# A third weight chunk at the feed-forward entries, and all first modulation blocks on VectorE, in a two-block float32 kernel

## The reference

```python
def modulated_norm(x, g, shift, scale):
    return rmsnorm(x, g) * (1 + scale) + shift
def swiglu(h, wg, wu, wd):                      # wg, wu: 1024 x 2816, wd: 2816 x 1024
    return (jax.nn.silu(h @ wg) * (h @ wu)) @ wd
def first_block(x, c, ...):
    c_act = jax.nn.silu(c)
    for l in range(2):
        mod = (c_act @ w_ada[l] + b_ada[l]).reshape(b, 9, 1, 1024)   # w_ada[l]: 1024 x 9216
        sh1, sc1, g1, sh2, sc2, g2, sh3, sc3, g3 = [mod[:, i] for i in range(9)]
        h = modulated_norm(x, norm_g[l, 0], sh1, sc1)
        x = x + 0.5 * g1 * swiglu(h, ffn_wg[l, 0], ffn_wu[l, 0], ffn_wd[l, 0])
        x = x + g2 * mixer(modulated_norm(x, norm_g[l, 1], sh2, sc2))
        x = x + 0.5 * g3 * swiglu(modulated_norm(x, norm_g[l, 2], sh3, sc3), ...)
    return x
```

## Time and profile before

| what | value |
|---|---|
| median of 3 runs | 2608.23 us (2608.07 to 2612.12) |
| the profiled execution: its time, its span | 2614.62 us, 2613.0 us |
| TensorE matmul, weight load | 2478.3 us (95%), 2118.1 us (81%) |
| VectorE, ScalarE, GpSimd busy | 1630.6 us (62%), 1080.0 us (41%), 315.1 us (12%) |
| DMA | 479.26 MB, 183 GB/s over the span |

### The profile page before, as it was taken

How to read it: one execution, slowest core, us unless ns; L and a number is a source line. 1 busy time by engine, 2 the same in 40 slices (tenths; PEclk the granted TensorE clock), 3 DMA queues, 4 the chain that set the end, 5 groups by cost and what they waited for, 6 DMA issues and landing times.

```text
span 2613.0 us, 35873 instructions
## 1 busy us (share of the span) xinstructions
PE 2478.3 (95%) x13317; PEld 2118.1 (81%) x13317; DVE 1630.6 (62%) x1759; ACT 1080.0 (41%) x1223; POOL 315.1 (12%) x425
## 2 busy tenths in 40 slices
PE   7999988999999899999998999899999999998998
PEld 7777857887888788888798888788788898887886
DVE  3887347767875555555566675645545657757455
ACT  3434335435434444444353334344344344254443
POOL 3110111101102000000005500000100016200000
PEclk9999979999999999999999999999999999999999
DMA  7996318967974466556543233556456331534554
GB/s 288 320 329 224 132 33 279 306 218 278 325 257 146 152 227 208 176 182 201 156 122 97 99 114 139 168 189 213 148 193 218 94 108 62 164 114 145 178 191 145
DMA packets 337379, 479.26 MB, mean 183 GB/s; under 512 B 19867, under 2 KB 280314, under 8 KB 337258
## 3 DMA queue, kind: packets, MB, share of 16 engines
q1 hardware_dynamic: 314458, 398.43, 46.6%
q0 software_dynamic: 22800, 79.23, 8.2%
HBM read 476.55 MB, written 1.05 MB: 183 GB/s over the span
## 4 chain that ended last, share of the span: by engine, by line
issue 53%; PE 33%; POOLq 5%; DVE 3%; POOL 2%; DMA 2%; ACT 1%; DVEq 1%; ACTq 0%
PE ps L920 10%; PE ps L922 10%; PE ps L921 10%; POOLq L891 3%; POOLq L895 2%; DVE w_lo L2030 1%; PE ps L1182 1%; POOL n_rstd L716 1%; DMA probs<-in_w_ada_dram 1%; DMA spare<-in_w_ada_dram 1%; PE ps L986 1%; DVE mix_mem L2133 1%; PE ps L1241 1%; ACT w_hi L1613 0%; POOL rstd L710 0%
## 5 line engine op out<-in xcount | busy, mean ns | idle before, releaser
L2030 DVE TENSOR_TENSOR w_lo<-raw,w_hi 128x2048 fp32r<-128x2048 f32 (+1 forms) x368 | 825.6, 2245 | 476.0 <-ACT w_hi L1613 472.3
L1613 ACT ACTIVATE w_hi<-raw 128x2048 fp32r<-128x2048 f32 (+1 forms) x368 | 689.0, 1873 | 386.9 <-PE ps L922 353.5
L920 PE MATMUL ps<-w_hi,x_hi 128*128 128x512 f32 x1424 | 571.6, 401 | 13.3 <-DVE x_lo L2042 7.7
L922 PE MATMUL ps<-w_hi,x_lo 128*128 128x512 f32 x1424 | 559.9, 393 | 0.0
L921 PE MATMUL ps<-w_lo,x_hi 128*128 128x512 f32 x1424 | 559.8, 393 | 0.0
L920 PE MATMUL ps<-x_hi,w_hi 128*128 128x256 f32 (+1 forms) x1152 | 338.3, 294 | 14.7 <-DVE w_lo L2030 11.9
L921 PE MATMUL ps<-x_lo,w_hi 128*128 128x256 f32 (+1 forms) x1152 | 331.1, 287 | 0.0
L922 PE MATMUL ps<-x_hi,w_lo 128*128 128x256 f32 (+1 forms) x1152 | 331.0, 287 | 0.0
L920 PEld LDWEIGHTS ps<-w_hi,x_hi 128*128 128x128 f32 x1424 | 270.8, 190 | 70.5 <-issue 10.4
L922 PEld LDWEIGHTS ps<-w_hi,x_lo 128*128 128x128 f32 x1424 | 270.6, 190 | 58.6
L921 PEld LDWEIGHTS ps<-w_lo,x_hi 128*128 128x128 f32 x1424 | 271.3, 190 | 54.1 <-issue 0.5
(11 more groups left out here) (403 smaller groups left out, 3085.5 us busy)
## 6 DMA issues: line engine op xcount, KB each, us to landing
raw<-in_w_in_dram SPq DMA_DIRECT2D x96, 512.0 KB, 4.6
raw<-in_ffn_w_gate_dram SPq DMA_DIRECT2D x90, 512.0 KB, 4.0
raw<-in_ffn_w_up_dram SPq DMA_DIRECT2D x90, 512.0 KB, 4.9
raw<-in_ffn_wg_dram SPq DMA_DIRECT2D x88, 512.0 KB, 4.6
raw<-in_ffn_wu_dram SPq DMA_DIRECT2D x88, 512.0 KB, 6.1
raw<-in_ffn_wd_dram SPq DMA_DIRECT2D x80, 512.0 KB, 4.9
raw<-in_ffn_w_down_dram SPq DMA_DIRECT2D x80, 512.0 KB, 4.0
spare<-in_w_ada_dram POOLq DMA_DIRECT2D x46, 512.0 KB, 6.5
```

The lines of the kernel that those rows point to most:

```text
L920: pe.matmul(dst, wh, vh, start=start, stop=False, skip_group_check=True)
L922: return pe.matmul(dst, wl, vh, start=False, stop=stop_, skip_group_check=True)
L1613: f(w_hi[s][:, 0:n], raw[s][:, 0:n], ACT.Copy).then_inc(hi_ready, 1)
L2030: v.tensor_tensor(w_lo[s][:, 0:n], raw[s][:, 0:n], w_hi[s][:, 0:n].bitcast(F32), ALU.subtract)\
```

## The change

**At entries.** A new argument `third` is true for seven of the eight feed-forwards, and false for the first. With it TensorE's order is A0, B0, the transposes, C0, A1, B1, C1. On ScalarE `silu(0, 0)` and on VectorE `made(0, 0)` come before `back()` instead of after it.

**At the start.** VectorE takes all sixteen units, through six buffers. TensorE sums a block after its eighth unit with matmuls against `ones`, the first block before and the second after `turn_x` and six new matmuls of 512 columns (identity with a tile of zeros, result not used) which wait for unit 12. GpSimd makes its constants ahead of its first DMA and has no drain between the DMAs. `quads` is made by VectorE, together with the constants that it made between its units before, now after the second chunk conversion. The conversion of chunk A on VectorE stands behind `mod_ready`. SyncE loads chunk A after unit 10 and chunk B after unit 16 instead of after the fourth and the eighth unit of VectorE.

```diff
@@ SyncE, ffn_start
-                    sp.wait_ge(ada_used, 4)
+                    sp.wait_ge(ada_used, 10)
                 load_gu(wg, wu, 0, 0)
-                    sp.wait_ge(ada_used, 8)
+                    sp.wait_ge(ada_used, 16)
                 load_gu(wg, wu, 0, 1)
@@ GpSimd
-            for u in range(LANDINGS):
-                first_unit(u, False)
-                first_unit(u, True)
...
+            for u in range(2 * KT):
+                if u >= ADA_SLOTS:
+                    pool.wait_ge(ada_used, u - ADA_SLOTS + 1)
+                ada_unit(u // KT, u % KT, landing(0, u)[0])
+                if u == 10:
+                    norm_power(0)
@@ TensorE, ffn
-                turn_x(c, 1, src)
+                if not third:
+                    turn_x(c, 1, src)
                 s1 = take(1)
                 x_ready(c, 0, 1)
                 gate_up(s1, 1, 0).then_inc(gu_ready, 1)
+                if third:
+                    turn_x(c, 1, src)
+                    s2 = take(2)
+                    made(0, 0)
+                    gate_up(s2, 0, 0)
                 x_ready(c, 1, 0)
                 used(gate_up(s0, 0, 1))
                 x_ready(c, 1, 1)
                 used(gate_up(s1, 1, 1))
 
-                pair(1, True)
+                pair(1, True, begun=third)
@@ TensorE, start
+            first_sums(0)
+            turn_x(0, 0, xn)
+
+            pe.wait_ge(ada_used, KT + 4)
+            for _ in range(6):
+                pe.matmul(ps[:, 3, :], ident[:], flat(vpad)[:, 0:512], start=True, stop=True)
+            first_sums(1)
+            ffn(0, 0, xn, xn, 1, third=False)
@@ VectorE, ffn (ScalarE alike with silu)
                 ahead(b + 3)
+                if third:
+                    made(0, 0)
                 back()
-                made(0, 0)
+                if not third:
+                    made(0, 0)
@@ VectorE, start
+            for u in range(2 * KT):
+                ada_unit(0, u)
                 dve.drain()
...
             dve.drain().then_inc(mod_ready, 1)
+            ahead(1)
             x_lo_a(0, 0)
             ahead(2)
+
+            v.tensor_reduce(quads[:, 0:32], ident[:].rearrange("p (c n) -> p n c", n=32), AX, ALU.add)
+            v.tensor_copy(ident_b[:], ident[:])
...
```

More of the change, by code:

```diff
@@ L252, in block_kernel @@
         ada_used = sem("ada_used")
[L253 removed]
+        cols_summed = sem("cols_summed")
         ada_reduced = sem("ada_reduced")
@@ L1015, in gates, with pair @@
                         gate_sum(grp, n)
-                def pair(i, first=False, with_gates=False):
+                def pair(i, first=False, with_gates=False, begun=False):
                     s = take()
-                    made(i - 1, 0)
-                    gate_up(s, 0, 0)
+                    if not begun:
+                        made(i - 1, 0)
+                        gate_up(s, 0, 0)
                     made(i - 1, 1)
@@ L1178, in _, with first_sums @@
             pe.transpose(ps[:, 0, 256:328], b_rows[:, 1, :], ident[0:72, 0:72]).then_inc(rows_turned, 1)
-            def first_sums(m, src, rhs, first=False):
+            def first_sums(m):
+                pe.wait_ge(ada_used, KT * m + KT)
                 for t in range(KT):
[L1182 to L1197, removed]
+                    last = pe.matmul(ps[:, 2, KT * m + t:KT * m + t + 1], ada_acc[:, m, t * P:t * P + P], ones[:, 0:1],
+                                     start=(m == 0 and t == 0), stop=True, skip_group_check=True)
+                last.then_inc(cols_summed, 1)
+            first_sums(0)
[5 more added lines that the diff above has]
+            ffn(0, 0, xn, xn, 1, third=False)
             def mix_a0():
@@ L1652, in rounded_x, with ffn @@
                     f(x_hi[:, 4 * half:4 * half + 4, t * P:t * P + P], turned_x(t, half), ACT.Copy).then_inc(x_hi_ready, 1)
-            def ffn(f_no, b, back, front=None, back_next=None):
+            def ffn(f_no, b, back, front=None, back_next=None, third=True):
                 def silu(i, t, n):
@@ L1670, in ffn @@
                 ahead(b + 3)
+                if third:
+                    silu(0, 0, None)
                 back()
-                silu(0, 0, None)
+                if not third:
+                    silu(0, 0, None)
                 ahead(b + 4)
@@ L1801, in a_ffn @@
                 if c < 5:
-                    ffn(f_no, A_FFN[f_no], lambda: modulated(c, 1), norm_front(c + 1), lambda: modulated(c + 1, 0))
+                    ffn(f_no, A_FFN[f_no], lambda: modulated(c, 1), norm_front(c + 1), lambda: modulated(c + 1, 0),
+                        third=c > 0)
                 else:
@@ L2189, in mod_finish, with ffn @@
                 dve.drain().then_inc(mod_ready, 1)
-            def ffn(f_no, b, back, border, grp=None, params=None):
+            def ffn(f_no, b, back, border, grp=None, params=None, third=True):
                 def made(i, t):
@@ L2330, in _ @@
             dve.drain().then_inc(cols_ready, 1)
[L2331 to L2335, removed]
-                dve.drain()
[L2337 to L2358, removed]
+            dve.wait_ge(c_ready, 1)
+            for u in range(2 * KT):
+                ada_unit(0, u)
+                dve.drain()
+                if u in (3, 4):
+                    square_moment(0, u - 3)
+            dve.wait_ge(cols_summed, 2)
             v.tensor_tensor(mod[:, 0:2, :].rearrange("p m t -> p (m t)"), ps[:, 2, 0:2 * KT], b_cols[:, 0, 0:2 * KT],
@@ L2364, in _ @@
             dve.drain().then_inc(mod_ready, 1)
+            ahead(1)
             x_lo_a(0, 0)
             ahead(2)
+            v.tensor_reduce(quads[:, 0:32], ident[:].rearrange("p (c n) -> p n c", n=32), AX, ALU.add)
+            v.tensor_copy(ident_b[:], ident[:])
+            v.tensor_copy(cmask_b[:], cmask)
+            v.tensor_copy(win[0][:, 0, :], count_i[:])
+            dve.drain()
+            v.tensor_copy(quads[:, 32:P].rearrange("p (c n) -> p c n", n=32), bc(quads[:, 0:32].unsqueeze(1), (P, 3, 32)))
+            v.reciprocal(win[1][:, 0, :], win[0][:, 0, :])
+            dve.drain()
+            for n, width in enumerate(WINDOWS):
+                v.tensor_scalar(inv_count[:, n, :], win[1][:, 0, :], 1.0 / width, None, ALU.max)
             dve.wait_ge(params2_in, 9 * 16)
@@ L2412, in a_ffn @@
             def a_ffn(f_no, c, grp):
-                ffn(f_no, A_FFN[f_no], lambda: x_lo_a(c, 1), border_a(c + 1, f_no) if c < 5 else border_6, grp)
+                ffn(f_no, A_FFN[f_no], lambda: x_lo_a(c, 1), border_a(c + 1, f_no) if c < 5 else border_6, grp,
+                    third=c > 0)
             a_ffn(0, 0, 1)
```

32 lines of the change are left out of this document (7 added, 25 removed).

## The result

| | before | after |
|---|---|---|
| time, median of 4 runs | 2608.4 us | 2635.4 us |
| profiled execution / its span | 2614.6 / 2613.0 us | 2631.9 / 2630.2 us |
| mean granted clock | 0.973 | 0.970 |

The ratio is 1.0099, 95% interval 1.0077 to 1.0122: 26 us slower, from 20 to 32. The forecast was +12 us and 2620 us, in a range of 2603 to 2630. The direction was right, the size was not, and the time lies outside the range.

A forecast was written before the change was run, and what follows sets the result against it. TensorE, busy for 95% of the span, was taken to bound the kernel, so time won or lost at an entry reaches the end. Entries +22 and start -10 gave +12 us: 2620 us, range 2603 to 2630.

The forecast's parts named there:

- the start, -10 us: Kernel start into the first feed-forward: earlier sums bring A0 and A1 forward, winning 10 us; bounds -4 and -13.
- (e): At the start, VectorE makes constants between the rests of B and C, costing 1.8 us: A1 at 50.6 instead of 60.46.
- Entries, +22 us: Seven feed-forward entries: new order costs 7.7 us without the clock and 14 by it, +22, between +8 and +28.
- First step: Entries, where C0 can start: doing C0 ahead of A1 uses part of the wait, winning 7.0 us together.
- Second step: Entries, ahead of C1: C0 no longer hides the wait for `made(0, 1)`, 2.1 us at all seven, 14.7 us lost.
- Third step: Entries, the clock: idle gaps cut in two or three bring more low-clock stretches, +14 us, bounds 0 and 20.
- the first stretch: Entries: one low-clock stretch for C0 or A1 at the six entries with such a gap, 9.0 us.
- the second: Entries: half a chance of another low-clock stretch behind C1's wait at all seven, 5.3 us.
- 1 (the clock stays high): At entries the clock stays high, so they cost 8 us; with the start's -10 the time is 2606 us; chance 0.17.
- 2 (faster): First feed-forward: a late-unit wait and low clock go, giving -17 us; with the entries' 8, 2599 us; chance 0.10.
- 3: The start gives only -4 us, its bound; with the entries' +22 the time is 2626 us; chance 0.23.

The follow-up runs named there:

- last start kernel: Kernel before with new start, old entry order, constants ahead of chunk B's rest, second token half ahead of chunk C, chunk B issued after unit 12: ratio 0.9975.
- entries-only kernel: Only the new entry order at seven entries, with the old start, against the kernel before: ratio 1.0085, +22 us.
- start-only kernel: Only the new start, with the old entry order everywhere, against the kernel before: ratio 1.000 (0.999 to 1.001).

## Why the prediction was wrong

- **The step that failed: the start, -10 us.** It gave 0 (-2.6 to +2.6). Up to A0 each step held: last unit at 31.4 (forecast 31.5), bias add at 34.2 (35.5), A0 at 39.70 (39.7). What failed is "B is the first and wanted from 40 on, C from 44: no further delay taken". The sum of bytes gave 43 us for the last of them, and B landed at 46.15 and C at 49.14, with SyncE held for 5.35 us at the issue of C's second transfer, and for 4.09 us at D's first. B0 then waited 3.98 us. Worse, the working looked at when B0 and C0 want their chunks, not at what stands behind the conversions: the second token half does, on both engines. The constants of (e) were taken to delay A1 by 1.8 us and lasted 4.1. In all A1 is at 57.88 instead of 50.6. The last start kernel, which removes just these three (the constants, chunk C ahead of the second half, B's late issue), puts A1 at 50.93 and gives -6.5 us, inside the forecast's bounds.
- **Low clock at the start.** A0 and B0 run 5.3 us each there. A0's isn't what cost the gain: A0 took 5.3 us before, too, and the kernel that fills the wait ahead of A0 has its C0 at 63.05 and a ratio of 1.0013. B0's costs nothing in the changed kernel, where A1 waits a further 1.96 us behind it. It counts once the constants are out of the way: A1 follows B0 with no wait there (49.09 to 54.32, 5.2 us), and in the last start kernel B0 takes 2.9 us. No run changed B0's clock alone.
- **Entries, +22 us: right**, by the total of the entries-only kernel (+22) and by the lengths (+22.9). First step, forecast -7.0: with the waits filled, A1 - A0 sums to 96.97, against 85.45 + 7 x 2.72 = 104.5 before, -7.5. Of these, 1.1 are the entry at 1855 (forecast 0.5), which wasn't filled, and at 602 it is 0.2 and not 0.7: chunk B's rest is late there, which the prediction, taking 602 for a copy of 405, didn't look at. Second step, forecast 7 x 2.1 = 14.7: measured 14.1, and `made` first on VectorE takes half of it away, as the lower bound of 1.1 us an entry said. Third step, forecast +14: A1 - A0 is 12.1 us longer unfilled than filled, 9.1 without the entry at 1855 (forecast 9.0). Behind C1 2.6 us come in the same way (4.2 beyond the first two steps after, 1.6 filled; forecast 5.3). That makes 11.7 us, or 14.7 with 1855. So the first stretch was sized about right and the second was rarer than taken, and that the sum comes out so close, +22 and +22.9, is in part luck.
- The shortest idle gap that the Trainium skill gives for a fall of the clock (TensorE: Matmul & The Clock Gate, HAM oscillation) would have made this third step some 3 us by the prediction's estimate. Here the clock fell behind a wait of 2.15 us (the shown C0 at 1673), and in the kernel before behind 1.80 us (1855: 1.00 up to 1855.5, 0.54 from 1855.6 on). The term measured 11.7 us or more; the measurement decides against the page's gap.
- **Rivals.** 1 (the clock stays high) and 2 (faster) are out. 3 came nearest, with the start at its low bound of -4 and 2626 us; the start fell even short of that bound. The bound priced the summing matmuls and an overlap of the transfers, and nothing behind A0.
- **What is not settled.** The two parts measured apart add to +22 us, the change itself to +26 (20 to 32). The intervals overlap; whether there are 4 us more in their meeting isn't known. The changed kernel's four runs lie at 2631, 2632, 2639 and 2639 us, and no experiment was made on that. With four runs a few us can be chance: 35 runs of the kernel before on one chip lie between 2606.8 and 2620.4 us.

## What to carry to other kernels

A matmul group that fills one wait was mostly the cover of another: before it is moved, list for each engine what its old place hid, and look there for the next wait. An earlier start of a stage is worth what its latest operand is worth, and that operand may be late only because an in-order engine has a conversion of something else ahead of it; count bytes for the transfer, then read the queue of each engine behind it. Where a wait can't be removed, cheap matmuls that end just before the operand comes kept the clock up here. They pay only if real work follows and no second wait does.

## What the runs showed of the hardware

The clock can fall while the profile counts TensorE as busy. These are the same instructions, in the first mixer, of the start-only kernel and of the changed kernel:

```profile
299.00:304.00 5.00, 5.00 (x25) 5.00 (x25) 0.19 (x1) 0.00 (x0) 3.34 (x1) 0.50 0.01 4
```

```profile
300.00:305.00 5.00, 5.00 (x43) 5.00 (x43) 0.19 (x1) 0.00 (x0) 4.62 (x1) 1.00 0.00 0
```

Both are busy for all of 5.00 us with no wait ahead of them, yet one is granted 0.50 and runs 25 matmuls where the other runs 43. From the mixer's first transposes to the next (253.19 to 313.83, and 253.97 to 311.54) it is 60.6 against 57.6 us. What stands ahead of both is a group of very narrow matmuls, with two moving columns each (L1217, 32 records): from 295.66 for 4.69 us in the start-only kernel, whose clock fell within the group (1.00 from 296 to 298, 0.50 from 298 to 300), and from 296.44 for 3.63 us in the changed kernel, whose clock stayed high. In the kernel before the group takes 3.63 us, and the clock is 0.55 right behind it (306 to 308). So "busy" in the profile does not say that the clock will hold; whether the narrow matmuls are the cause was not tested. Of the fifteen traces of this case, five have the group at 3.63 us and ten between 3.70 and 4.85. A landmark late in one trace therefore says less than the ratio of many runs.

At the very start the clock's column is no guide: A0 of the earlier trace rows lies in this stretch of the kernel before,

```profile
51.30:56.60 5.30, 5.24 (x12) 4.02 (x13) 4.39 (x7) 3.68 (x3) 0.00 (x0) 1.00 1.00 380
```

whose column says 1.00, while it takes 5.3 us for 12 matmuls: one every 0.43 us, the low rate, instead of 0.23.

A transfer's issue on SyncE, 0.3 to 0.5 us as a rule here, took 5.35 and 4.09 us while the DMA engines were full (380 GB/s from 36 to 46 us). Transfers can then be not only slow to land but late to be issued, and a sum of bytes from the first issue doesn't show it. Full engines alone don't explain it: from 20 to 30 us they moved 370 GB/s, and the two issues of chunk A, at 22.50 and 22.93, took 0.38 and 0.51 us. At 32.90 SyncE had issued three transfers since 31.39; whether that is the cause was not tested.
